# GpSimd issues the loads of the weight slabs itself in a two-layer hybrid backbone

## What is computed

```python
for l in range(DEPTH):
    sh1, sc1, g1, sh2, sc2, g2 = split(silu(c) @ w_mod[l] + b_mod[l], 6)      # and the same of c_ctx
    hx = rmsnorm(x) * (1 + sc1) + sh1                                         # and hc of ctx
    y_x = token_mixers(hx @ w_in[l], ...)     # retention, Fourier mixing, gated convolution
    x = x + g1 * (y_x @ w_out[l])
    x = x + g2 * conv_ffn(rmsnorm(x) * (1 + sc2) + sh2, ffn_w_up[l], ffn_conv_w[l], ffn_w_down[l])
    # in layer 0 the context rows take the same path
return rmsnorm(x, final_norm_g)
```

## Time and profile before

| what | us |
|---|---|
| median of 3 runs | 1689.31 |
| lowest and highest of them | 1688.16, 1696.31 |
| span of the profiled execution (first to last instruction) | 1692.4 |

### The profile page before, as it was taken

The page is one execution under the profiler, slowest core; times in us unless marked ns, Lnnn a source line. Parts: engine busy times, 40 slices in busy tenths (PEclk is TensorE's granted clock), DMA queues, the critical chain, the costliest instruction groups (busy, mean ns, idle before and its releaser), DMA issues.

```text
span 1692.4 us, 23806 instructions
## 1 busy us (share of the span) xinstructions
PE 1618.0 (96%) x8620; PEld 1344.0 (79%) x8620; DVE 953.3 (56%) x1310; ACT 326.4 (19%) x489; POOL 806.6 (48%) x636
## 2 busy tenths in 40 slices
PE   8989999989899999999999999999989999999997
PEld 2778788778778888888888888877767787887876
DVE  2797554277787875884288648454456441341445
ACT  2502111230312200220022214111221220120220
POOL 1144232275344454444444444452465666676664
PEclk9899999999899999999999999999999999999998
DMA  8244111233133243331333222221122222222222
GB/s 345 95 153 165 45 38 38 68 135 131 62 124 125 100 154 124 118 136 64 110 124 112 90 97 77 87 86 50 63 75 87 85 89 98 91 95 99 99 87 99
DMA packets 49633, 174.42 MB, mean 103 GB/s; under 512 B 6448, under 2 KB 6832, under 8 KB 48560
## 3 DMA queue, kind: packets, MB, share of 16 engines
q1 hardware_dynamic: 45504, 167.79, 28.1%
q10 hardware_dynamic: 4080, 5.94, 1.3%
HBM read 167.41 MB, written 2.10 MB: 100 GB/s over the span
## 4 chain that ended last, share of the span: by engine, by line
PE 52%; DVE 16%; issue 13%; POOL 8%; DMA 7%; ACT 2%; DVEq 1%; ACTq 0%; POOLq 0%; SPq 0%
PE pair L1005 43%; DMA raw<-in_slabs 6%; POOL w_lo L384 5%; DVE aux L616 3%; POOL w_hi L382 2%; PE pair L1054 2%; DVE tg L947 2%; DVE tv L947 2%; PE aux L1210 1%; DVE hid_lo L975 1%; PE aux L1181 1%; PE aux L1196 1%; DVE modv L619 1%; PE aux L1215 1%; DVE tv L972 1%
## 5 line engine op out<-in xcount | busy, mean ns | idle before, releaser
L1005 PE MATMUL pair<-h_hi,w_hi 128*128 128x512 f32 x1888 | 572.0, 361 | 20.2 <-POOL w_lo L384 12.3
L1005 PE MATMUL pair<-h_lo,w_hi 128*128 128x512 f32 x1888 | 563.9, 356 | 7.2 <-DVE h_lo L721 5.5
L1005 PE MATMUL pair<-h_hi,w_lo 128*128 128x512 f32 x1888 | 563.8, 356 | 0.0
L384 POOL TENSOR_TENSOR w_lo<-raw,w_hi 128x1024 fp32r<-128x1024 f32 x210 | 535.1, 2548 | 17.5
L380 POOL TENSOR_TENSOR gate<-ones 128x1 f32<-128x1 f32 x210 | 56.3, 268 | 848.4 <-PE pair L1005 753.7
L1005 PEld LDWEIGHTS pair<-h_hi,w_hi 128*128 128x128 f32 x1888 | 311.4, 191 | 75.8 <-issue 18.2
L1005 PEld LDWEIGHTS pair<-h_lo,w_hi 128*128 128x128 f32 x1888 | 311.4, 190 | 66.7 <-DVE h_lo L721 13.3
L1005 PEld LDWEIGHTS pair<-h_hi,w_lo 128*128 128x128 f32 x1888 | 312.3, 191 | 49.6
L616 DVE CUSTOM_DVE_ANT_0 aux<-mod_slot,c_b 128x1024 f32<-128x1024 f32 x160 | 231.3, 1445 | 5.6 <-DMA mod_slot<-in_mods 2.8
L382 POOL TENSOR_SCALAR w_hi<-raw 128x1024 fp32r<-128x1024 f32 x210 | 223.4, 1064 | 0.1
L1005 PE MATMUL pair<-hid_hi,w_hi 128*128 128x512 f32 (+1 forms) x528 | 160.6, 358 | 5.6 <-POOL w_lo L384 4.9
(11 more groups left out here) (137 smaller groups left out, 1129.7 us busy)
## 6 DMA issues: line engine op xcount, KB each, us to landing
raw<-in_slabs SPq DMA_DIRECT2D x210, 512.0 KB, 3.2
mod_slot<-in_mods SPq DMA_DIRECT2D x80, 512.0 KB, 3.2
start_slot<-in_start_mods SPq DMA_DIRECT2D x8, 1024.0 KB, 13.8
x<-in_x SPq DMA_DIRECT2D x4, 768.0 KB, 18.2
rot<-kT ACTq DMA_DIRECT2D x32, 64.0 KB, 2.0
rot<-Y ACTq DMA_DIRECT2D x32, 64.0 KB, 2.0
out<-fin SPq DMA_DIRECT2D x8, 256.0 KB, 2.2
c_b<-in_c SPq DMA_DIRECT2D x1, 512.0 KB, 4.2
```

The costliest lines, as they stand in the source:

```text
L384: nc.gpsimd.tensor_tensor(w_lo[p][:, :], raw[p][:, :], w_hi[p][:, :].bitcast(fp32), ALU.subtract).then_inc(split, 1)
L1005: ins = nc.tensor.matmul(out[:, a:b], wt, xt[:, a:b], start=first and k == 0, stop=last and k == 2)
```

## The change

The slab loads leave SyncE's list and go to GpSimd. GpSimd issues slabs 0 and 1 at its very start, and slab s+2 right after it has split slab s, into the buffer that this split has freed. Between the split and the load stands a wait for its own split and a second tiny multiplication `gate`. SyncE keeps start blocks, constants, modulation blocks and stores; the modulation blocks keep their order and their waits on `mod_used`.

```diff
@@ block.sync @@
-            def load_slab(s, p):
-                sp.dma_start(raw[p][:, :], io["slabs"][s, :, :]).then_inc(loaded[p], 16)
-            def load_slabs(first, n):
-                with sp.Fori(0, n) as i:
-                    for p in range(2):
-                        sp.wait_ge(split, 2 * (first + p - 1) + 4 * i)
-                        load_slab(first + p + 2 * i, p)
...
-            load_slab(0, 0)
-            load_slab(1, 1)
...
-            for n_mods in MODS_KVQ:
-                load_slabs(s, 1)
+            for j, n_mods in enumerate(MODS_KVQ):
...
             for g, n in enumerate(GROUPS):
-                with sp.Fori(0, n - 1) as i:
+                with sp.Fori(0, n) as i:
                     for p in range(2):
-                        sp.wait_ge(split, 2 * (s + 1 + p) + 4 * i)
-                        load_slab(s + 2 + p + 2 * i, p)
                         sp.wait_ge(mod_used, m + p - 1 + 2 * i)
                         sp.dma_start(mod_slot[p][:, :], io["mods"][2 * i + (m + p), :, :])\
                             .then_inc(mod_loaded[p], 16)
...
@@ block.gpsimd @@
+            def load_slab(s, p):
+                pool.dma_start(raw[p][:, :], io["slabs"][s, :, :]).then_inc(loaded[p], 16)
+
-            def split_slab(p, n, first):
+            def split_slab(p, n, first, last):
...
+                if not last:
+                    pool.wait_ge(split, 4 * n + (2 * p + 2))
+                    nc.gpsimd.tensor_tensor(gate[:, 1:2], ones[:, 0:1], ones[:, 0:1], ALU.mult).then_inc(gate_done, 1)
+                    pool.wait_ge(gate_done, 1)
+                    load_slab(2 * n + (2 + p), p)
             for p in range(2):
-                split_slab(p, 0, True)
-            with pool.Fori(1, PLAN["end"] // 2) as i:
+                load_slab(p, p)
+            for p in range(2):
+                split_slab(p, 0, True, False)
+            with pool.Fori(1, PLAN["end"] // 2 - 1) as i:
                 for p in range(2):
-                    split_slab(p, i, False)
+                    split_slab(p, i, False, False)
+            for p in range(2):
+                split_slab(p, PLAN["end"] // 2 - 1, False, True)
```

More of the change, by code:

```diff
@@ L153, in build_program @@
     ones = new("ones", [P, 1])
-    gate = new("gate", [P, 1])
+    gate = new("gate", [P, 2])
     root_probe = new("root_probe", [P, 1])
@@ L311, in _ @@
                 sp.dma_start(dst, src).then_inc(consts_loaded, 16)
-            s, m = 2, 0
-            for n_mods in MODS_KVQ:
-                load_slabs(s, 1)
-                if s == 2:
+            m = 0
+            for j, n_mods in enumerate(MODS_KVQ):
+                if j == 0:
                     sp.wait_ge(start_turned, 2)
@@ L322, in _ @@
                 load_mods(m, n_mods)
-                s, m = s + 2, m + n_mods
-            load_slabs(s, (PLAN[0, "out"] + 2 - s) // 2)
+                m += n_mods
             sp.wait_ge(S[0]["o_ready"], NLC + NCC)
[L326 to L329, removed]
+            load_mods(m, MODS_OUT * KB // 2)
+            m += MODS_OUT * KB // 2
             for g, n in enumerate(GROUPS):
-                s = PLAN[0, "up", g]
-                if g == 2:
-                    load_slabs(s, 1)
-                with sp.Fori(0, n - 1) as i:
+                with sp.Fori(0, n) as i:
                     for p in range(2):
-                        sp.wait_ge(split, 2 * (s + 1 + p) + 4 * i)
-                        load_slab(s + 2 + p + 2 * i, p)
                         sp.wait_ge(mod_used, m + p - 1 + 2 * i)
@@ L340, in _ @@
                             .then_inc(mod_loaded[p], 16)
[L341 to L358, removed]
+                m += n * MODS_UP
+                if g == 0:
+                    load_mods(m, MODS_OUT * KB // 2)
+                    m += MODS_OUT * KB // 2
+            load_mods(m, MODS_LAST * 2)
+            m += MODS_LAST * 2
             assert MOD_START + m == n_mod
-            load_slabs(s + 2, (PLAN["end"] - s - 2) // 2)
             for k in range(KB):
```

## The result

| what | before | after |
|---|---|---|
| median, us (20 runs of each, side by side) | 1689.84 | 1698.87 |
| lowest and highest | 1684.69, 1696.31 | 1692.30, 1702.33 |
| profiled execution: span (time) | 1692.4 | 1697.0 (1699.23) |

The account below looks back on a forecast made before the run. TensorE, busy 1618 of 1692 us, was taken as the bound, so only its waits count. The terms -8.2 + 6.4 + 2.0 + 0 + 2.5 gave +2.7 us, a median of 1692.0 us, with a range of 1684 to 1718.

Parts of the forecast that it names:

- (a): Layer 0's late slab loads: four TensorE gaps and a clock loss vanish, VectorE's longer wait absorbing the shift: -8.2 us.
- rival 3: Layer 0 projections: VectorE bounds them, so only 3.1 us come off; 1697 us; chance 0.06.
- (b): GpSimd's added price per slab: wait and gate together 0.25 us, issue 1.05; total 1.3, bounds 0.6 and 2.65.
- A: Price of one slab on GpSimd (split wait, second gate, issue): 1.3 us, 1.6 where VectorE also reads SBUF.
- (c): Layer 0's short slabs around the Fourier stage: nothing hides GpSimd's added cost, four turns of 1.6 us: +6.4 us.
- (d): Layer 1's short slabs: two turns before the first output slab lengthen, partly hidden by a gap: +2.0 us.
- (e): Long slabs of both layers: GpSimd's pauses cover the added cost, thinly in layer 1: 0 us.
- Rival 1: Layer 1: GpSimd becomes the bound if an issue costs over 1.3 us; 1708 to 1750 us; chance 0.26.
- (f): Kernel start: 2 MB of early slab loads delay the start blocks, partly absorbed by slack: +2.5 us (0 to 5).
- the slack of 2.3 us: Kernel start: seventh start block lands at 27.6 and is needed near 29.9, so 2.3 us of delay are free.
- (g): Modulation blocks go out once their buffer is free, never behind an unready slab; stores stay last: 0 us.
- Rival 2: GpSimd's issue is held another 1.0 us where VectorE is busy: in all +11 us, 1700 us; chance 0.07.

Follow-up runs that it names:

- e2: The kernel before, but GpSimd issues only slabs 4 to 13, the stage of the late loads: 1685.02 us, ratio 0.9963 to before.
- e10: Repeat of e2 (only slabs 4 to 13 issued by GpSimd, all else as before): 1686.39 us, ratio 0.9970 to before.
- e1: The changed kernel, but the Fourier slabs' loads (28 to 33, 134 to 139) back on SyncE: 1692.33 us, ratio 1.0005 to before.
- e6: The changed kernel measured again, unaltered: 1697.88 us, ratio 1.0049 to before.
- e9: The kernel before, but GpSimd issues slabs 142 to 209, layer 1's feed-forward stage: 1694.12 us, ratio 1.0012 to before.
- e7: The changed kernel with two more gates behind each issue: 1702.16 us, ratio 1.0066 to before.
- e8: The changed kernel with five more gates behind each issue: 1739.49 us, ratio 1.0296 to before.
- e3: The changed kernel, but slabs 0 to 3 issued by SyncE at their old places: 1693.80 us, ratio 1.0019 to before.
- e4: The changed kernel without the second gate, the issue itself waiting for the split: 1696.06 us, ratio 1.0028 to before.
- e12: The kernel before, all loads on SyncE, with 1, 3, 3, 3, 4, 2 modulation blocks between slab pairs: 1684.96 us, ratio 0.9969 to before.

## Why the prediction came out as it did

**(a) Late loads, predicted -8.2, measured -5.7** by the ratios of e2 and e10, whose intervals reach from 2.4 to 9.0, and 7.0 to 7.2 in their traces from slab 2 to 24. The gaps went as predicted: no wait for a low part in the stage, and 8.6 to 9.0 us won at slab 12. The step that failed is "the later, longer wait can take up the whole gain, so it passes on". VectorE did take most of it up, but TensorE then waited 4.2 us for ScalarE's copy of k at 160. In e2's timeline ScalarE makes that copy after its four rotary issues, and these follow VectorE's rotary additions; that is rival 3 in part. Between slabs 12 and 24, 1.2 to 2.6 us are given back.

**(b) A, predicted 1.3, measured 1.27 to 1.31.** That was luck: two errors cancel. The issue takes 0.61 and not the 1.05 that I took from the high part, and 0.66 us, not 0.25, pass between low part and issue, of which 0.40 are dead time that I hadn't counted.

**(c), (d) The short slabs, predicted +8.4, measured +6.6** (e1; give or take 2.7). Layer 0 is what I overpriced: 6.4 forecast, 4.2 to 4.6 lost in the traces of e6 and of the changed kernel. The turns grew by 1.13 us there rather than 1.6: of the four second gates only one was stretched (0.19, 0.19, 1.01, 0.19), and the turns of before, 4.0 against 3.7 without a stretch, held some stretching already. In layer 1 the loss was 3.3 in the first trace, 1.5 of it from the clock, and 1.8 in e6's, against 2.0 forecast.

**(e) Long slabs, predicted 0,** 0.5 at most in the traces of the changed kernel, e6 and e9 over layer 1's feed-forward stage (slab 142 to 202); the cover is as thin as forecast (e7, e8). The ratio of e9 leaves up to a few microseconds open. Rival 1 had the right mechanism and the wrong price: it needed an issue over 1.3 us, and e8 shows what it would have been: A near 2.1 to 2.5 there and 50 us over before, where the rival gave 61 for 2.25. (Its 1718 for an issue of 1.6 us, the upper end of the range, comes out at 1715 to 1717 by its own terms.)

**(f) The start, predicted +2.5, measured +4.6 and +4.2** by ratios, 3.5 by the mean of traces. The landing was right: the seventh block lands at 5.9 + 26.5 = 32.4, 4.8 later than the 27.6 of the earlier trace rows. The step that failed is the slack of 2.3 us. I took it from a phase ending at 33.80, and that phase was long because its matmuls ran partly at the lower clock. In e2 it ends at 32.0, the last eight matmuls take 3.6, so the seventh block is needed at 32.0 - 3.6 = 28.4 and lands at 5.5 + 21.7 = 27.2: the slack is 1.2. I had also priced one block, while the blocks before it came late too.

**(g) Modulation blocks, 0:** VectorE waits for them hardly longer than before, though with two queues they land in 4.0 us instead of 3.2.

**The sum** with measured terms: -5.7 + 6.6 + 4.6 = +5.5, and 0 to 2 for (e), against 7.4 (5.7 to 9.3) measured. The 4.7 us missed are mostly (a) and (f), +2.5 and +2.1, less 1.8 for (c) and (d); the last 1.9 lie within the intervals of the runs, e9's among them. Each of these terms is known to two or three microseconds only, so their order is shown and their sizes are not sharp. Rival 2, an issue held up by VectorE, did not happen: all 210 took 538 to 746 ns. What was stretched is the second gate, up to 1.23 us; of the gates of 0.6 us and more, first and second, 49 of 68 lie beside a dot product of VectorE. One issue of the 208 started only after 2.6 us of idle time, at 1060.31. Each of the seven kernels that issue almost all slabs from GpSimd has one such between 1057 and 1105 us, in e3 (3.1 us) while VectorE does nothing, so its cause is another and open.

**What stays open:** what e4 gains; whether the covered issues cost a few microseconds; what an unrolled issue would save. e12's trace goes on gaining after slab 24 while its ratio doesn't, but its profiled execution was the fastest of its six (1680.04, 4.9 under their median), so no more is to be read from it.

## What to carry to other kernels

When one queue serves two consumers, a wait for the slow one holds back the loads of the fast one; look for the order first, because moving a load ahead in the list cost nothing here, while issuing from GpSimd in a loop charged it 1.3 us for each load. Price such a cost where the issuing engine has no pause (here the 10 Fourier slabs of 210), and where early transfers meet a saturated queue, not by the mean busy share. A slack read from one execution is only as good as that execution's clock: check the duration of equal instructions in it before you subtract.

## What the runs showed of the hardware

- An issue on GpSimd (128 rows of 4 KB) occupied it for 0.61 us against 0.33 on SyncE's queue. In a loop it started 0.66 us after the end of the instruction that it had to wait for, with a short gate between them or none; outside the loop 0.30 us. The transfer landed 3.6 us after its issue from GpSimd and 3.2 from SyncE.
- Beside VectorE's dot products GpSimd's gate took up to 1.23 us for 0.19, but its issue never more than 0.75 for 0.61. The Trainium skill ("SBUF — State Buffer", Who interferes with whom) says that a VectorE operation with both inputs in SBUF contends with GpSimd's reads. The stretched gates agree. It also says (the same page, SBUF: two separate sides) that a two-port mode of VectorE keeps GpSimd from writing descriptors. No run here shows that.
- It goes both ways. VectorE's dot products between 70 and 170 us, before and after, took 1324 and 1594 ns; with GpSimd loading only in this stage (e2) 1494:

```profile
L616 DVE CUSTOM_DVE_ANT_0 aux<-mod_slot,c_b 128x1024 f32<-128x1024 f32 x32 | 42.4, 1324 | 3.4 <-DMA mod_slot<-in_mods 2.8
```

```profile
L595 DVE CUSTOM_DVE_ANT_0 aux<-mod_slot,c_b 128x1024 f32<-128x1024 f32 x32 | 51.0, 1594 | 3.7 <-DMA mod_slot<-in_mods 3.2
```

- With transfers running at 410 to 425 GB/s, 2 MB more in front cost TensorE 4.2 to 4.6 us by the ratios (3.5 by the mean of the traces), most of the 5.0 that they take.
